# A recurrence in chunks on one core: a new timetable for its preparation, Gram products and output, and preparation products on both row halves

## The reference, cut to what matters

```python
w_log = -softplus(-(w0 + einsum('bsdr,drc->bsdc', tanh(lw), w2))) - 0.5
decay = heads(exp(-exp(w_log)))
iclr = heads(sigmoid(a0 + einsum('bsdr,drc->bsdc', la, a2)))
...
def step(state, inp):
    r_t, w_t, k_t, v_t, kk_t, a_t = inp
    sa = einsum('bhij,bhj->bhi', state, -kk_t)
    state = (state * w_t[:, :, None, :] + sa[..., None] * (kk_t * a_t)[:, :, None, :]
             + v_t[..., None] * k_t[:, :, None, :])
    return state, einsum('bhij,bhj->bhi', state, r_t)
...
y = direction(0, False) + direction(1, True)
```

## Time and profile before

| | |
|---|---|
| median of three runs | 3922.16 us (3920.52 to 3924.79) |
| the profiled execution | 3922.59 us, its span 3920.8 us |
| PE busy | 3759.4 us, 96% of the span |
| DVE, ACT, POOL busy | 43%, 37%, 35% |
| granted clock of PE, mean over the span | 0.99 |

### The profile page before, as it was taken

How to read it: one execution, slowest core, us unless ns; L and a number is a source line. 1 busy time by engine, 2 the same in 40 slices (tenths; PEclk the granted TensorE clock), 3 DMA queues, 4 the chain that set the end, 5 groups by cost and what they waited for, 6 DMA issues and landing times.

```text
span 3920.8 us, 67096 instructions
## 1 busy us (share of the span) xinstructions
PE 3759.4 (96%) x28976; PEld 3041.0 (78%) x28976; DVE 1679.8 (43%) x2714; ACT 1438.2 (37%) x2442; POOL 1382.9 (35%) x581
## 2 busy tenths in 40 slices
PE   8888999999999899999999999999999999999999
PEld 7677768888887776687888876778888777788887
DVE  6554441487145554612683167415111376332112
ACT  3354252323233443522223243634222436434222
POOL 5000324444442002144444454233444353244443
PEclk9999999999999999999999999999999999999999
DMA  3001212266221001132473221112222221122222
GB/s 145 2 4 46 83 60 102 86 248 231 86 89 42 4 4 66 68 113 86 161 274 133 93 101 65 44 65 102 90 104 86 105 89 34 63 98 86 86 108 86
DMA packets 37150, 356.65 MB, mean 91 GB/s; under 512 B 4224, under 2 KB 4352, under 8 KB 17920
## 3 DMA queue, kind: packets, MB, share of 16 engines
q1 hardware_dynamic: 19584, 278.93, 19.3%
q10 hardware_dynamic: 17280, 73.48, 5.2%
HBM read 350.29 MB, written 2.10 MB: 90 GB/s over the span
## 4 chain that ended last, share of the span: by engine, by line
PE 84%; DVE 7%; ACT 3%; issue 2%; DMA 1%; POOL 1%; PEld 1%; PEldq 0%; DVEq 0%; SPq 0%; ACTq 0%; POOLq 0%
PE banks L762 23%; PE banks L764 23%; PE banks L763 23%; PE banks L1121 10%; PE banks L2166 3%; ACT arena L2319 1%; DMA ring<-stream 1%; ACT arena L1484 1%; PE banks L2248 1%; DVE arena L1964 1%; PE banks L1230 1%; DVE arena L1858 0%; DVE x L2706 0%; POOL ring_r L860 0%; PE banks L1436 0%
## 5 line engine op out<-in xcount | busy, mean ns | idle before, releaser
L860 POOL TENSOR_TENSOR ring_r<-ring,hi_ring 128x1024 fp32r<-128x1024 f32 x490 | 1201.6, 2456 | 2206.9 <-ACT hi_ring L851 2206.6
L762 PE MATMUL banks<-xT_r,ring_r 128*128 128x512 f32 (+1 forms) x2480 | 953.8, 385 | 13.4 <-POOL ring_r L860 6.9
L764 PE MATMUL banks<-xT_r,hi_ring 128*128 128x512 f32 x2096 | 828.4, 395 | 0.0
L763 PE MATMUL banks<-x_lo_r,hi_ring 128*128 128x512 f32 x2096 | 824.1, 393 | 0.0
L851 ACT ACTIVATE hi_ring<-ring 128x1024 fp32r<-128x1024 f32 x490 | 511.2, 1046 | 731.8 <-DMA ring<-stream 301.0
L762 PEld LDWEIGHTS banks<-xT_r,ring_r 128*128 128x128 f32 x2480 | 470.4, 190 | 109.6 <-issue 15.9
L764 PEld LDWEIGHTS banks<-xT_r,hi_ring 128*128 128x128 f32 x2096 | 395.6, 189 | 94.2
L763 PEld LDWEIGHTS banks<-x_lo_r,hi_ring 128*128 128x128 f32 x2096 | 397.7, 190 | 89.9 <-issue 3.4
L1121 PE MATMUL banks<-arena 64*64 64x64 f32 (+4 forms) x7456 | 351.5, 248 | 53.3 <-DVE arena L1858 23.8
L1484 ACT ACTIVATE arena<-banks 128x512 f32<-128x512 f32 x366 | 214.7, 595 | 404.7 <-PE banks L764 242.8
L764 PE MATMUL banks<-hi_ring,pairs 128*128 128x512 f32 x864 | 342.3, 396 | 0.0
(11 more groups left out here) (263 smaller groups left out, 5462.8 us busy)
## 6 DMA issues: line engine op xcount, KB each, us to landing
ring<-stream SPq DMA_DIRECT2D x132, 2048.0 KB, 7.7
arena<-ada ACTq DMA_DIRECT2D x96, 512.0 KB, 4.7
arena<-ln_rows ACTq DMA_DIRECT2D x5, 1024.0 KB, 8.2
arena<-edge ACTq DMA_DIRECT2D x4, 1024.0 KB, 5.0
arena<-edge ACTq DMA_DIRECT2D x2, 1792.0 KB, 8.3
arena<-pack ACTq DMA_DIRECT2D x2, 1485.0 KB, 6.8
arena<-pack ACTq DMA_DIRECT2D x2, 1200.5 KB, 5.5
x<-x_in SPq DMA_DIRECT2D x4, 512.0 KB, 7.3
```

What stands on the lines that cost most here:

```text
L762: first = nc.tensor.matmul(out_, left[1], right[0], start=start, stop=False)
L763: low = nc.tensor.matmul(out_, left[0], right[1], start=False, stop=False)
L764: return first, low, nc.tensor.matmul(out_, left[0], right[0], start=False, stop=stop)
L860: nc.gpsimd.tensor_tensor(feed.raw(n, ring_r), feed.raw(n), feed.hi(n).bitcast(F32), ALU.subtract).then_inc(split_lo, 1)
```

## The change

It rewrites the slots of a group, and with them the banks of some steps.

- `prep_w` comes in the slot of `prep`, `prep_a` one slot later, and `prep_b` with `prep_ar` two slots earlier than before. The Gram products stay in slot 7 and move from 8 to 9, and stand now between `inv_a` of a level and its `inv_x` (levels 2 and 3 of the group before). `prep` writes banks 4 and 5.
- The transposes, `x0`, the levels and the output go one to three slots down; `oo` and the first link share a slot. A group has 36 slots instead of 33.
- `oo` makes its first half, then the state-free parts of links 1 and 0, then its second half; before, the first link made these two behind `oo`.
- `v_rows` takes bank b1 and `turned` 0 bank b0, where both took bank 6.
- The product with a2 reads the other 64 rows than the product with w2. For this the two halves of 64 in `z[13]`, in a2 and in the two shift factors of that tile are swapped in the layout outside the chip.

```diff
-    turned = [("v_rows", j, (6,))] if d == 0 else []
-    out = [[("prep", g, (b0, b1))], [], [("prep_w", g, ())], [], [("prep_a", g, ())], [], [("prep_b", g, ()), ("prep_ar", g, ())],
-           [("gram", g, 0, (b0, b1))], [("gram", g, 1, (b0, b1)), ("unit", g, ())], [("turned", g, 0, (6,))] + turned,
-           [("x0", g, (b0,)), ("turned", g, 1, (b1,))], [("turned", g, 2, (6,))]]
+    rows_ = [("v_rows", j, (b1,))] if d == 0 else []
+    out = [[("prep", g, (4, 5)), ("prep_w", g, ())], [("prep_a", g, ())], [], [], [("prep_b", g, ()), ("prep_ar", g, ())], [], [],
+           [("gram", g, 0, (b0, b1))], [], [("gram", g, 1, (b0, b1)), ("unit", g, ())], [("turned", g, 0, (b0,))] + rows_,
+           [("turned", g, 1, (b1,))], [("x0", g, (b0,)), ("turned", g, 2, (6,))], [], []]
...
-    out += [[("wu", g, (b0, b1))], [("mq", g, (b0, b1))], [("oo", g, ())]]
-    out += [[("link", g, i, (4 + i % 2,) if i < NC - 1 else ())] for i in range(NC)]
+    out += [[("wu", g, (b0, b1))], [("mq", g, (b0, b1))], []]
+    out += [([] if i else [("oo", g, ())]) + [("link", g, i, (4 + i % 2,) if i < NC - 1 else ())] for i in range(NC)]
...
-                    h = slice(64 * d, 64 * d + 64)
+                    h = side((d, 1 - d)[which])
...
-                    pe.wait_ge(halves_done, halves(g) + p_)
+                    if p_:
+                        for m in (1, 0):
+                            ahead(g, m)
+                    pe.wait_ge(halves_done, halves(g) + 2 * p_)
...
-                for m in (0, 1) if i == 0 else (i + 1,) if i + 1 < NC - 1 else ():
...
+                if 0 < i < NC - 2:
+                    ahead(g, i + 1)
```

More of the change, by code:

```diff
@@ L1133, in begin, with ahead @@
             return n > 0 and n not in (3, 4)
+        def ahead(g, m):
+            (b,), (b_use,) = uses[("link", g, m)]
+            d, j = g % 2, g // 2
+            c = (m, NC - 1 - m)[d]
+            q, h = c // 2, side(c % 2)
+            take(b, b_use)
+            for n in range(2):
+                for e in range(2):
+                    left, right = ((GM[d][h, q, e, 1, 2, :], V[j % 2][h, q, e, :]), (GM[d][h, q, e, 0, 2, :], WU[d][h, q, e, 1, :]))[n]
+                    ins = mm(bank[b][side(e), 0:CH], left, right, n == 0, n == 1 and m == 0)
+            ins.then_inc(*((halves_done, 1) if m else (bank_full[b], 1)))
         def step(name, *args):
@@ L2842, in columns_of, with sides_swapped @@
     return v.reshape(-1, P).T
+def sides_swapped(a):
+    return np.concatenate([a[CH:], a[:CH]])
 def first_units(i, l):
@@ L2847, in first_units @@
     zr = 4 * S
-    wz = np.concatenate([w[:, zr + P * t:zr + P * t + P] for t in Z_ORDER], axis=1)
+    wz = np.concatenate([sides_swapped(w[:, zr + P * t:zr + P * t + P].T).T if t == 13 else w[:, zr + P * t:zr + P * t + P]
+                         for t in Z_ORDER], axis=1)
     out = [unit_rows(wz[:, c:c + 512], 512) for c in range(0, ZT * P, 512)]
@@ L2864, in first_pack @@
     rep = lambda a: np.broadcast_to(a.reshape(1, -1), (P, a.size))
-    parts = [i["rw_w2"][l].reshape(P, 512), i["rw_a2"][l].reshape(P, 512), i["rw_g2"][l], rep(i["da_lambda"][l]), np.full((P, 1), lam_init, np.float32),
+    parts = [i["rw_w2"][l].reshape(P, 512), sides_swapped(i["rw_a2"][l].reshape(P, 512)), i["rw_g2"][l], rep(i["da_lambda"][l]), np.full((P, 1), lam_init, np.float32),
              np.full((P, 1), 1.0 - lam_init, np.float32)]
@@ L2868, in first_pack @@
                  "rw_gn_g", "rw_gn_b", "da_subln_g"):
-        parts.append(columns_of(i[name][l].reshape(-1)))
+        columns_ = columns_of(i[name][l].reshape(-1))
+        if name in ("rw_mu_prev", "rw_mu_next"):
+            columns_ = np.concatenate([columns_[:, :13], sides_swapped(columns_[:, 13:14]), columns_[:, 14:]], axis=1)
+        parts.append(columns_)
     parts.append(i["pool_w"][l].transpose(1, 0, 2).reshape(P, 512))
```

## The result

The changed kernel took 3935.1 us (median of six runs, 3933.1 to 3943.3), the kernel before 3918.8 us beside it; the ratio is 1.0046, with a 95% interval of 1.0035 to 1.0057. The forecast was 3908 with a range up to 3922: the change makes the kernel slower by about half a per cent, and the prediction was wrong in its sign. The profiled execution took 3936.1 us, 13.5 more than that of before.

What follows compares the result with a forecast made beforehand. PE, busy 96% of the span, was taken as the bound, so removed PE waits win time. Per layer, -11.7 periods, -2.2 tail, -0.8 projections, +3.1 and +4.5 front gave -7.1; two layers -14.2, so 3908 us, range 3893 to 3922.

Steps and rivals of the forecast that it cites:

- 12 periods: Six recurrence periods per layer, each 4.0 us saved less 2.05 of new waits: 1.95 shorter, 27.7 us.
- the rest: Group 0's product pair among the projections, where PE has no pause: 0.8 us saved per layer.
- The front: Group 0's first mask waits behind DVE's preparation: PE stands 6.4 us; 3.1 lost plus 4.5 for low clock, per layer.
- Rival A: The front's pause costs no clock, or low clock ends at once: 3899 us; chance 20%.
- The tail: After the last period, `gram` 1 already done and several waits gone, less 0.9 for `mq`: 2.2 us saved per layer.
- The new waits: Per period, `mq` waits 0.9 us for `wu`'s second copy, `inv_x` 0 a mean 1.15 for level 0's mask: 2.05 added.
- Rival C: The preparation's two products still go one after the other: 3922 us, no change; chance 12%.
- its 0.85 us: The preparation's product pair on two row halves takes 1.13 us instead of 1.98: 0.85 saved per period.
- The waits that go: Per period, PE's waits removed at `gram` 0 (0.8 us), levels 2 and 3 (1.4), `wu` (0.3) and `v_rows` (0.4 mean).
- 0.67 + 0.78 = 1.4: Inverse levels 2 and 3: `gram` 0 and 1 fill the mask waits before `inv_x`, saving 1.4 us per period.
- the 0.8 of `gram` 0: At `gram` 0, the input now ends two slots earlier, so its wait goes: 0.8 us saved per period.
- Rival B: New pauses at `mq` and `inv_x` 0 lower the clock inside periods: 3935 us, or 3962 with all twelve; chance 13%.

Runs made afterwards that it cites:

- e6: e2 with group 1 alone prepared as in the old timetable (old front): 3895.3 us, ratio 0.9942 to the kernel before.
- e5: Changed kernel with the preparation's two products back on the same 64 rows, so the new timetable alone: 3939.2 us, ratio 1.0054 to the kernel before.
- h1: Changed kernel with half the instructions in some inverse steps, same columns, part of the computation left out: 3915.3 us, ratio 0.9984 to the kernel before.
- h0: Kernel before with the same halved instructions as h1: 3908.6 us, ratio 0.9968 to the kernel before.
- h8: h1's halving on e7 with `turned` 2 moved between `wu` and `mq`: 3870.5 us, against 3894.9 us without the halving.
- e3: Changed kernel with `gram` 0 one slot later, so level 2's mask is waited for again: 3941.7 us, ratio 1.0046 to the kernel before.
- e2: Changed kernel with `prep_a` behind level 0's mask, `prep_b` and `prep_ar` behind level 1's: 3905.0 us, ratio 0.9958 to the kernel before.
- e7: e6 with the preparation's product pair two slots earlier, behind `turned` 0 in the dense stretch: 3897.0 us, ratio 0.9927 to the kernel before.

## Why the prediction was wrong, point by point

The forecast was -14.2 us for the profiled execution; it was +13.5, so 27.7 us are to be found. From the landmarks of both recurrences:

| | forecast | measured |
|---|---|---|
| two fronts (gram 0 to r0 0) | +15.2 | +16.3 |
| 12 periods | -23.4 | +6.0 |
| two tails (r0 6 to the end) | -4.4 | -6.0 |
| the rest (pair of group 0 among it) | -1.6 | -2.8 |

**The front was right**, in size and cause: 6.77 us of idle time at `inv_x` 0 for L1866 (forecast 6.4), a second stretch at 1.2 GHz, and +8.0 and +8.3 us in the two layers (forecast 7.6). Rival A, the front without the clock's cost, is out. e6 shows that the loss can be undone.

**The tail was right** in sign, and near in size: -3.5 and -2.6 for -2.2.

**The new waits were right, one by one.** `mq`: 0.90 idle for 0.89. `inv_x` 0 starts 12.31 and 13.03 us after `r0`, by the d of the group prepared, forecast 12.1 and 12.8. The idle time there, 1.28 and 1.87, is above the 0.5 to 1.3 that I gave, more because PE came there earlier than reckoned (by some 0.4) than because DVE was later (by 0.2). Rival C is out: the pair is issued in 1.06 us. But e5 shows that its 0.85 us did little in this timetable, since the chain of DVE starts at its first product; I had added it to the sum and the DVE wait beside it, which is right for the sum and hides that the two cancel.

**The waits that go were right, and their worth was wrong.** `gram` 0, levels 2 and 3, `wu` and `v_rows` lost their waits as forecast. The step that failed is "0.67 + 0.78 = 1.4" for levels 2 and 3, with the 0.8 of `gram` 0: I took each wait in the dense stretch for time on the path. The stretch was to take 11.3 us and took 13.25; that is 1.95 x 12 = 23 of the 29.4 us that the periods miss. Without its pauses it would be right: in the first recurrence the six periods hold 11.5 us of them, 1.9 each, and 12.92 - 1.92 is 11.0. Before, they hold 3.8. In the second recurrence it is the same: 15.2 us of pauses, 2.5 each, and 13.58 - 2.54 is 11.0 again. What bounds the stretch is not PE's columns and not DVE's masks but some 3.9 us for every 256 instructions. h1, h0 and h8 show it; in e3 the stretch stays as long with a wait put back. It was to be seen in the earlier trace rows: the 1.60 us with "issue" behind it are such a pause, and I used that row as evidence about the clock without asking what the pause was.

**Rival B was half right.** The clock does fall inside the periods, in five of the 12: four times after the 1.87 us at `inv_x` 0, once after the 1.3 us of the other kind. By the stretch from `inv_x` 0 to `inv_x` 1, 4.29 for 3.87, it cost 5 us in all, where B had 27: a fall lasts some 3.4 us there and not the 10 us of the front. I had set the Trainium skill, "TensorE: Matmul & The Clock Gate", section "A second HAM failure mode: psum-queue depth-cycling", against the row of the tail and followed the row; in these periods the trace agrees with the page: the granted clock went to 0.50 and back to 1.00 in five of the 12. The time came out at B's 3935 by accident: B's mechanism gave 5 of the 27.7 us.

The remaining 2 us of the periods are `inv_x` 0 starting 0.2 later than forecast. Two sums of the prediction are a little off in themselves, without weight for the result: group 0's levels start 143.0 - 137.2 = 5.8 us late by its own numbers, not 6.0, and 5.4 with 7.3 or 6.6 gives 12.7 or 12.0, not 12.8 or 12.1. What sets the 1.2 to 1.6 us between the end of a packet and PE's going on was not tried, nor why the clock falls in some periods and not in others.

## What to carry to other kernels

Before a wait between short instructions is counted as time to be won, count the instructions around it: look at the queue of kind "instruction", divide the records by its packets, and compare the fastest spacing of those packets with the time in which the stretch would use one up. Where the stretch is already near that, fill the waits of other stretches first (e2 kept 22 of the 22.8 us that it took out there). Work with few instructions, moved into such a stretch behind its pauses, took nothing from them (e7). And when an engine's work is moved ahead, look at the first round, where the cover of the steady state isn't there yet: the front lost 8 us in each layer, as much as the six periods of e6 gain on those of before (7.7).

## What the runs showed of the hardware that I had not expected

- PE's instructions come as packets of 16.4 KB, one for 256 records of PE, PEld and sequencer, and at the 34 stops of the changed kernel the next was fetched only when PE had gone on with the last: 3.5 to 4.2 us a piece, in the median 3.9, where PE uses one up in 1.9. It stops at the same 256th places in every kernel, and the wait is shown as "issue".
- Halving the number of matmuls at the same columns left the step's time almost as it was (0.46 to 0.50 us for 0.49 to 0.53) and still gave 10 to 24 us, while the pauses fell by 12 to 23.
- After a wait of 1.9 us the clock fell for some 3.4 us in some periods and not in others of the same order; after the 6.8 us of the front it was low for 13.6 us.
